# One unread TensorE product behind each unit of a written-out expert layer, in a two-block transformer kernel

## The chip, the cores and the metric

The kernel runs on one core of a Trainium2 chip, as one program launch. The metric is the device time of that launch in microseconds, and what is compared is the median of several runs. TensorE does the matrix products, ScalarE (ACT) and VectorE (DVE) the elementwise work and the reading of PSUM, GpSimd (POOL) one kind of subtraction, and the SyncE queue (SP) issues the loads of weights.

## What is computed

The reference runs two transformer blocks over 256 tokens of width 2048: a first one with matrix LSTM scan, pooling and a gated unit, and a second one with attention, a recurrent branch and a layer of experts. Around the change it is the experts that matter:

```
def peer_ffn(x, w_peer_q, peer_subkeys, peer_u, peer_v):
    ...
    def chunk(args):
        xc, ec, gc = args
        u = peer_u[ec]
        act = jax.nn.gelu(jnp.einsum('tkd,td->tk', u, xc))
        return jnp.einsum('tk,tkd->td', gc * act, peer_v[ec])
```

There are 16384 experts. Each token picks 128 of them (8 heads by 16), and the kernel computes the first expert layer, `gelu(peer_u @ x)`, for all experts and all 256 tokens, then weights the result with a mostly empty table of gates, and multiplies by `peer_v`.

## The kernel before

All weights come through one stream of **units** of 2048 columns by 128 partitions (1 MB). SP loads a unit into one of four `ring` buffers. A unit marked N is split for accuracy: ACT copies each half to `unit_hi` (rounded to the fp32r form that TensorE reads in one pass), POOL subtracts to give `unit_lo`, and TensorE makes three products for each piece of 128 columns: hi by hi, hi weights by lo tokens, lo weights by hi tokens. There are four hi and four lo half-unit buffers, so the split runs up to two units ahead. The semaphores are `hi_done` (ACT to POOL), `lo_done` (POOL to PE), `half_done` (PE to ACT, which also frees the buffers) and `tile_free` (the reader of a PSUM bank to PE).

`STAGES` lists the stages in program order, and `plan()` numbers their units. The experts are handled in two halves, r = 0 and r = 1. Each half has these stages:

- `peer_u{r}`: 64 units. Each unit makes one tile of 128 experts by 256 tokens, with 16 pieces of three products, so 48 products of 256 columns. The tile goes to one of the PSUM banks 0 to 3 in turn. ACT applies the gelu and writes it into `peer_w`.
- for r = 1 only, `pp`: two units, a small projection that VectorE copies out.
- `build`: 32 groups of 16 products of 64 columns in banks 5 and 6 (the gate table, built from `hot` and `hotg`), which VectorE multiplies into `peer_w`.
- `peer_v{r}`: 64 units. Here all 16 pieces of output stay in PSUM over the whole stage, in all eight banks. VectorE then adds banks 0 to 7, one after the other, to `resid`. For r = 0 it raises `acc_used` after bank 3, and again after bank 7.

On TensorE, `run()` calls `iterations()`, which makes a loop (`Fori`) of 15 iterations of four units, and writes out the last four units behind it. Inside a unit, `n_unit()` waits for `lo_done` for each half, waits for `tile_free` before the first product, and raises `half_done` at the last product of each half. Before `peer_u1`, TensorE waits for `acc_used` of 1, since that stage writes banks 0 to 3 alone. It waits for `acc_used` of 2 before the `build` of r = 1. Other stages (`ro`, `wo`, `pq` among them) have patterns of 16 units that are written out, without a loop.

Of the kernel before, what the change touches and what calls it, by code (L numbers as in the profile page):

```python
# [32 lines left out]
P = 128  # L33
T = 256
D = 2048
KC = D // P
# [4 lines left out]
TILES = 4  # L41
# [10 lines left out]
I2 = NKEY // 2  # L52
# [2 lines left out]
NG = KC // GR  # L55
BIG = 3.0e38
GATE_UP = 2.0 ** 15
SCALE = 192.0 ** -0.5


# [100 lines left out]
PLAN, N_UNITS, N_SPLIT = plan()  # L161
# [12 lines left out]
def program(nc, A, out):  # L174
    with ExitStack() as ctx:
# [33 lines left out]
        bank = [ctx.enter_context(nc.psum_tensor(f"bank{i}", [P, 512], F32)) for i in range(8)]  # L209
# [3 lines left out]
        def S(name):  # L213
            if name not in sems:
                sems[name] = ctx.enter_context(nc.semaphore(name))
            return sems[name]
# [4 lines left out]
        tile_free = {"D": S("tile_free_dve"), "A": S("tile_free_act")}  # L221
# [18 lines left out]
        xl = [zone("xl_hi", 0, [P, KC, T], F32R), zone("xl_lo", 16, [P, KC, T], F32R)]  # L240
# [216 lines left out]
        def _(pe):  # L457
# [9 lines left out]
            def n_unit(s, movs, per_tile, it, j):  # L467


                n_tiles = s.tiles // len(movs)  # L470
                n = s.n0 + j + it * s.npi
                for f in range(2):
                    b = (2 * (s.n0 + j) + f) % NBUF
                    pe.wait_ge(lo_done, 2 * n + f + 1)
                    for i in range(8 * f, min(8 * f + 8, n_tiles * per_tile)):
                        t, k = i // per_tile, i % per_tile
                        if s.name == "pg" and j == 0 and k == 3 * GR:
                            ple_sums(0, 3)
                        if s.name in SPLITS and isinstance(it, int) and it == 0 and j == 0 and k % GR == 0:
                            moving_ready(s.name, k // GR)  # L480
                        tile = [(j * n_tiles + t) * len(movs) + m for m in range(len(movs))]
                        if k == 0:

                            pe.wait_ge(tile_free[s.eng], s.base + tile[-1] + 1 + it * (s.npi * s.tiles))
                        for w, x in ((hb, 0), (hb, 1), (lb, 0)):
                            for m, mv in enumerate(movs):
                                mm = pe.matmul(bank[(s.t0 + tile[m]) % TILES][:, 0:T],  # L487
                                               w[b][:, (i % 8) * P:(i % 8 + 1) * P], mv[x][:, k, :],
                                               start=(k == 0 and w is hb and x == 0),
                                               stop=(k == per_tile - 1 and w is lb))  # L490
                    mm.then_inc(half_done, 1)
# [30 lines left out]
            def run(name, movs=None, per_tile=KC, extra=None, mid=None, early=False):  # L522

                s = PLAN[name]

                if s.td:
                    pe.wait_ge(tile_free["D"], TILES + s.td)
                if s.ta and not early:
                    pe.wait_ge(tile_free["A"], TILES + s.ta)

                def body(it, last):
                    j = 0
                    for pos, kind in enumerate(s.pattern):
                        if kind == "P":
                            continue
                        n_unit(s, movs, per_tile, it, j)
                        if extra is not None:
                            extra(it, j)
                        j += 1
                iterations(pe, s, body, mid, 1 if name in SPLITS else 0)  # L540
# [123 lines left out]
            for d in range(2):  # L664
                for t in range(4):
                    mm = pe.matmul(bank[5][:, (d * 4 + t) * 4:(d * 4 + t) * 4 + 4],
                                   gi[:, t * P:(t + 1) * P], ident[0:64, 32 * d:32 * d + 4],
                                   start=True, stop=True, skip_group_check=True)
# [18 lines left out]
            for i in range(2 * NH):  # L687
                pick = ident[0:64, 32 * (i % 2) + i // 2:32 * (i % 2) + i // 2 + 1].to_broadcast([64, P])
                mm = pe.matmul(bank[4 + i // 2][:, (i % 2) * T:(i % 2 + 1) * T], pick, mrow[:], start=True, stop=True,
                               skip_group_check=True)  # L690
# [6 lines left out]
            for g in range(4):  # L697
                for j in range(2):
                    for k in range(2):
# [3 lines left out]
                                       start=(k == 0), stop=(k == 1), skip_group_check=True)  # L703
# [220 lines left out]
            pe.wait_ge(S("pu_ready"), NG)  # L924
            for r in range(2):
                if r == 1:
                    pe.wait_ge(S("acc_used"), 1)
                run(f"peer_u{r}", [xl], mid=(12, gates_tp) if r == 0 else None)
                if r == 1:
                    pe.wait_ge(S("p_ready"), 1)  # L930
                    run("pp", [[pt_r[:, 0, :, :], pt_r[:, 1, :, :]]], per_tile=2)


                def build(it, r=r):
                    for k in range(2):
                        i = r * (T // TG) + k + it * 2
                        pe.wait_ge(S("hot_1"), i + 1)
                        pe.wait_ge(S("hot_g"), i + 1)
                        pe.wait_ge(S("g_used"), i + 1)
                        for t in range(TG):  # L940
                            for x in range(2):
                                mm = pe.matmul(bank[5 + k][:, t * I2:(t + 1) * I2], oa[k][:, :, t], ob[k][:, x, :, t],  # L942
                                               start=(x == 0), stop=(x == 1), skip_group_check=True)
                        mm.then_inc(S("g_done"), 1)
                if r == 1:
                    pe.wait_ge(S("acc_used"), 2)
                with pe.Fori(0, T // TG // 2) as it:
                    build(it)

                s = PLAN[f"peer_v{r}"]  # L950
                pe.wait_ge(tile_free["A"], TILES + s.ta)
                pe.wait_ge(tile_free["D"], TILES + s.td)
                pe.wait_ge(S("g_used"), (r + 1) * (T // TG) + 2)

                def body(it, first, r=r, s=s):
                    for j in range(4):
                        n = s.n0 + j + it * 4
                        pe.wait_ge(S("wr_ready"), r * I2 + j + 1 + it * 4)
                        for f in range(2):
                            b = (2 * (s.n0 + j) + f) % NBUF  # L960
                            pe.wait_ge(lo_done, 2 * n + f + 1)
                            for c in range(8):
                                cc = 8 * f + c
                                o = bank[cc // 2][:, (cc % 2) * T:(cc % 2 + 1) * T]
                                for w_, x in ((hb, 0), (hb, 1), (lb, 0)):
                                    mm = pe.matmul(o, w_[b][:, c * P:(c + 1) * P], wr[j % 2][:, x, :],  # L966
                                                   start=(first and j == 0 and cc % 2 == 0 and w_ is hb and x == 0),
                                                   stop=False, skip_group_check=True)
                            mm.then_inc(half_done, 1)
                body(0, True)  # L970
                with pe.Fori(1, s.iters) as it:
                    body(it, False)
# [1535 lines left out]
```

## Time and profile before

| | |
|---|---|
| time before, median of 3 runs | 4004.07 us |
| lowest and highest of them | 3997.33 and 4007.48 us |
| span of the profiled execution | 3992.3 us |
| instructions in it | 73386 |
| TensorE products, and weight loads | 30508 each |
| PE busy (share of the span) | 3801.4 us (95%) |
| POOL busy | 2894.1 us (72%) |
| DVE busy | 1848.5 us (46%) |
| ACT busy | 1556.9 us (39%) |
| mean granted TensorE clock | 0.967 |

The profile is of one execution, from its first instruction to its last. The run time holds the span and what lies around it, so the table's median is higher than the span. The stage that is changed, `peer_u1`, stands in the span between 3049 and 3413 us.

### The profile page before, as it was taken

The page shows a single profiled execution, that of the slowest core. Times are in us where ns is not written, and L with a number is a line of the kernel's source. Part 1 is how long each engine was busy: PE and PEld are TensorE (multiplying, and loading weights), DVE is VectorE, ACT ScalarE, POOL GpSimd, SP SyncE. Part 2 cuts the span into 40 slices and gives each one's busy share as a digit, 9 for nine tenths or more (in the row PEclk, how much of TensorE's full clock was granted, in tenths as well). Part 3 has the DMA queues.
Part 4 walks back from the last instruction along what each step waited for, and adds up shares of the span by engine and source line. Part 5 has one row for each costly group of instructions (what it writes and reads, how often), then busy time and mean ns, then how long its engine had stood idle before and what let it go on. Part 6 is the DMA issues. An engine that isn't in the chain of part 4 may idle for free.

```text
span 3992.3 us, 73386 instructions
## 1 busy us (share of the span) xinstructions
PE 3801.4 (95%) x30508; PEld 3670.4 (92%) x30508; DVE 1848.5 (46%) x2576; ACT 1556.9 (39%) x1879; POOL 2894.1 (72%) x1146
## 2 busy tenths in 40 slices
PE   6999998899999889999999999999999999999988
PEld 3799998899998879999999999989999999899988
DVE  6685347773425464372025692264442100634445
ACT  5313433333434334454444334414444444144443
POOL 0157965686976738698888798828887888288876
PEclk9999999999999999999999999969999999699999
DMA  8466743463743425345555445515554555145543
GB/s 329 166 264 259 272 183 127 169 231 139 273 169 123 151 83 209 138 169 190 183 188 181 176 179 188 189 53 190 183 184 176 184 189 183 69 169 182 186 148 127
DMA packets 98248, 714.11 MB, mean 179 GB/s; under 512 B 11024, under 2 KB 11152, under 8 KB 12048
## 3 DMA queue, kind: packets, MB, share of 16 engines
q1 hardware_dynamic: 97056, 703.65, 48.2%
q10 hardware_dynamic: 1008, 7.79, 0.5%
q8 instruction: 141, 2.31, 0.2%
q14 instruction: 43, 0.35, 0.0%
HBM read 709.30 MB, written 2.10 MB: 178 GB/s over the span
## 4 chain that ended last, share of the span: by engine, by line
PE 75%; POOL 11%; DVE 8%; issue 3%; ACT 2%; DMA 1%; DVEq 0%; POOLq 0%; SPq 0%; ACTq 0%
PE bank L487 47%; PE bank L966 18%; POOL unit_lo L445 11%; PE bank L942 3%; PE bank L616 1%; DMA ring<-in_w 1%; DVE unit_lo L1582 1%; PE bank L516 1%; PE bank L555 1%; ACT unit_hi L988 1%; PE bank L499 1%; PE bank L725 0%; ACT att_s L1202 0%; PE bank L892 0%; DVE c_raw L1949 0%
## 5 line engine op out<-in xcount | busy, mean ns | idle before, releaser
L445 POOL TENSOR_TENSOR unit_lo<-ring,unit_hi 128x1024 fp32r<-128x1024 f32 x1132 | 2869.2, 2552 | 983.4 <-ACT unit_hi L988 982.0
L988 ACT ACTIVATE unit_hi<-ring 128x1024 fp32r<-128x1024 f32 x1204 | 1239.4, 1055 | 1238.8 <-PE bank L487 543.1
L487 PE MATMUL bank<-xl_hi,unit_hi 128*128 128x256 f32 x4976 | 1405.8, 283 | 50.8 <-POOL unit_lo L445 27.5
L487 PE MATMUL bank<-xl_hi,unit_lo 128*128 128x256 f32 x4976 | 1394.3, 280 | 0.0
L487 PE MATMUL bank<-xl_lo,unit_hi 128*128 128x256 f32 x4976 | 1393.7, 280 | 0.0
L487 PEld LDWEIGHTS bank<-xl_hi,unit_hi 128*128 128x128 f32 x4976 | 940.7, 189 | 62.4 <-issue 26.9
L487 PEld LDWEIGHTS bank<-xl_lo,unit_hi 128*128 128x128 f32 x4976 | 941.3, 189 | 0.5
L487 PEld LDWEIGHTS bank<-xl_hi,unit_lo 128*128 128x128 f32 x4976 | 941.5, 189 | 0.0
L966 PE MATMUL bank<-w_r,unit_hi 128*128 128x256 f32 x4096 | 728.2, 280 | 4.5 <-DVE w_r L2315 4.5
L966 PEld LDWEIGHTS bank<-w_r,unit_hi 128*128 128x128 f32 x4096 | 629.2, 189 | 5.0 <-issue 5.0
L966 PE MATMUL bank<-w_r,unit_lo 128*128 128x256 f32 x2048 | 574.3, 280 | 0.0
L2315 DVE TENSOR_TENSOR w_r<-peer_w,w_r 128x256 fp32r<-128x256 f32 x128 | 290.9, 2273 | 425.9 <-ACT w_r L1329 425.9
L966 PEld LDWEIGHTS bank<-w_r,unit_lo 128*128 128x128 f32 x2048 | 386.9, 189 | 0.0
L1406 DVE SCALAR_TENSOR_TENSOR ada_acc<-ring,cond,ada_acc 128x2048 f32<-128x2048 f32 x64 | 230.7, 3604 | 86.5 <-DMA ring<-in_w 84.9
L1318 ACT ACTIVATE peer_w<-bank 128x256 f32 (+1 forms) x128 | 49.4, 386 | 439.3 <-PE bank L487 439.3
L2296 DVE COPY ple_in<-bank 128x256 f32<-128x256 f32 x16 | 5.7, 418 | 313.2 <-PE bank L487 313.2
L487 PE MATMUL bank<-ry_hi,unit_hi 128*128 128x256 f32 x512 | 142.5, 278 | 2.9 <-DVE h_acc L2166 2.3
L487 PE MATMUL bank<-ry_hi,unit_lo 128*128 128x256 f32 x512 | 142.3, 278 | 0.0
L487 PE MATMUL bank<-ry_lo,unit_hi 128*128 128x256 f32 x512 | 142.1, 278 | 0.0
L487 PE MATMUL bank<-xc_hi,unit_hi 128*128 128x256 f32 x448 | 128.0, 286 | 10.0 <-DVE tick L1534 7.3
L942 PE MATMUL bank<-hotg,hot 128*128 128x64 f16 x1024 | 135.0, 301 | 1.8 <-issue 0.4
L942 PEld LDWEIGHTS bank<-hotg,hot 128*128 128x128 f16 x1024 | 120.2, 147 | 16.1 <-issue 16.1
(415 smaller groups left out, 4979.4 us busy)
## 6 DMA issues: line engine op xcount, KB each, us to landing
ring<-in_w SPq DMA_DIRECT2D x669, 1024.0 KB, 4.8
resid<-in_xT ACTq DMA_DIRECT2D x1, 2048.0 KB, 15.7
tmp_ctx<-in_ctxT ACTq DMA_DIRECT2D x1, 2048.0 KB, 10.6
rnn_gates<-in_rgw ACTq DMA_DIRECT2D x1, 2048.0 KB, 9.1
out<-resid SPq DMA_DIRECT2D x4, 512.0 KB, 2.6
con<-in_con ACTq DMA_DIRECT2D x1, 512.0 KB, 3.2
con<-in_con ACTq DMA_DIRECT2D x1, 448.0 KB, 7.9
p_tmp<-in_pT ACTq DMA_DIRECT2D x1, 256.0 KB, 4.0
```

The costliest lines, as they stand in the source:

```text
L445: pool.tensor_tensor(lb[b][:], ring[slot][:, f * HALF:(f + 1) * HALF], hb[b][:].bitcast(F32), ALU.subtract).then_inc(lo_done, 1)
L487: mm = pe.matmul(bank[(s.t0 + tile[m]) % TILES][:, 0:T], w[b][:, (i % 8) * P:(i % 8 + 1) * P], mv[x][:, k, :], start=(k == 0 and w is hb a ...
L499: mm = pe.matmul(bank[4][:, 64 + b * KC + c:65 + b * KC + c], a[:, c * P:(c + 1) * P], ones[:, 0:1], start=True, stop=True, skip_group_che ...
L516: mm = pe.matmul(bank[(s.t0 + 2 * (j // 4) + t) % TILES][:], xl[x][:, k, t * P:(t + 1) * P], w_[u][:, q * 512:(q + 1) * 512], start=(k == ...
L555: mm = pe.matmul(dst, ones, src[:, k, :], start=(k == 0), stop=(k == n - 1))
L616: mm = pe.matmul(dst[:, m * T:(m + 1) * T], w_[b][:, (i % 8) * P:(i % 8 + 1) * P], mv[x][:, k, :], start=(first and w_ is w[0] and x == 0 ...
L942: mm = pe.matmul(bank[5 + k][:, t * I2:(t + 1) * I2], oa[k][:, :, t], ob[k][:, x, :, t], start=(x == 0), stop=(x == 1), skip_group_check=True)
L966: mm = pe.matmul(o, w_[b][:, c * P:(c + 1) * P], wr[j % 2][:, x, :], start=(first and j == 0 and cc % 2 == 0 and w_ is hb and x == 0), sto ...
L988: act.activation(hb[b][:], ring[slot][:, f * HALF:(f + 1) * HALF], ACT.Copy).then_inc(hi_done, 1)
L1318: act.activation(at_chunk(W, j + it * 4), bank[(s.t0 + j) % TILES][:, 0:T], ACT.Gelu_apprx_tanh).then_inc(tile_free["A"], 1)
L1406: dve.scalar_tensor_tensor(a[:], ring[u % RING][:], col, a[:], ALU.mult, ALU.add).then_inc(plain_done, 1)
L2315: dve.tensor_tensor(wr[j % 2][:, 1, :], at(W, i), wr[j % 2][:, 0, :].bitcast(F32), ALU.subtract).then_inc(S("wr_ready"), 1)
```

## The change

A table `BESIDE` of 64 widths is added: 16 different widths from 8 to 252 columns, each four times, 6752 columns in all. For r = 1 the loop on TensorE is replaced by 64 calls of `n_unit` that are written out. Behind each unit stands one more product. Its weights are a piece of `xl_lo`, its moving operand the first columns of `xl_hi`, as many as the table says, and its result goes to bank 7, where nobody reads it. Since bank 7 is still to be read when `peer_v0` ends, the wait before the stage is now for `acc_used` of 2. No other engine's program is changed.

```
--- before.py
+++ after.py
@@ -55,6 +55,11 @@
+BESIDE = [8, 64, 128, 16, 96, 240, 32, 252, 48, 160, 192, 24, 224, 12, 80, 112,
+          128, 8, 240, 96, 16, 64, 252, 160, 32, 24, 48, 112, 192, 80, 224, 12,
+          96, 16, 8, 252, 128, 32, 64, 48, 240, 112, 24, 80, 160, 12, 192, 224,
+          64, 96, 160, 8, 48, 128, 24, 16, 112, 12, 252, 240, 32, 224, 80, 192]
...
@@ -924,9 +929,17 @@
             pe.wait_ge(S("pu_ready"), NG)
             for r in range(2):
                 if r == 1:
-                    pe.wait_ge(S("acc_used"), 1)
-                run(f"peer_u{r}", [xl], mid=(12, gates_tp) if r == 0 else None)
-                if r == 1:
+                    pe.wait_ge(S("acc_used"), 2)
+                if r == 0:
+                    run("peer_u0", [xl], mid=(12, gates_tp))
+                else:
+                    s = PLAN["peer_u1"]
+                    pe.wait_ge(tile_free["D"], TILES + s.td)
+                    pe.wait_ge(tile_free["A"], TILES + s.ta)
+                    for u in range(I2):
+                        n_unit(s, [xl], KC, u // 4, u % 4)
+                        pe.matmul(bank[7][:, 0:BESIDE[u]], xl[1][:, 0, 0:P], xl[0][:, 0, 0:BESIDE[u]],
+                                  start=True, stop=True, skip_group_check=True)
                     pe.wait_ge(S("p_ready"), 1)
                     run("pp", [[pt_r[:, 0, :, :], pt_r[:, 1, :, :]]], per_tile=2)
```

At the start of the stage, TensorE's program stood like this: the end of `peer_v0` (products from `w_r`), the branch into the loop with its waits, and the first product of the first unit.

```order
15028 L966 MATMUL bank<-w_r_180,unit_lo_60 128x256
15029 L971 REGISTER_ALU
15030 L971 COMPARE_AND_BRANCH
15031 L416 UNCONDITIONAL_BRANCH [waits tile_free_act,tile_free_dve,acc_used]
15032 L416 ISA
15033 L484 REGISTER_ALU [waits lo_done]
15034 L487 MATMUL bank<-xl_hi,unit_hi_53 128x256 [waits tile_free_act]
```

In the changed kernel the same place reads (L492 is the line that was L487, and L979 the one that was L966):

```order
15028 L979 MATMUL bank<-w_r_180,unit_lo_60 128x256
15029 L984 REGISTER_ALU
15030 L984 COMPARE_AND_BRANCH
15031 L492 MATMUL bank<-xl_hi,unit_hi_53 128x256 [waits lo_done,tile_free_act,tile_free_dve,acc_used]
15032 L492 MATMUL bank<-xl_lo,unit_hi_53 128x256
```

The branch and the register work are gone, and the waits stand at the first product. The end of the loop's fourth unit, with the jump back to the first, was this on TensorE:

```order
15233 L487 MATMUL bank<-xl_hi,unit_hi_56 128x256
15234 L487 MATMUL bank<-xl_lo,unit_hi_56 128x256
15235 L487 MATMUL bank<-xl_hi,unit_lo_60 128x256
15236 L416 REGISTER_ALU
15237 L416 COMPARE_AND_BRANCH
15238 L487 MATMUL bank<-xl_hi,unit_hi_53 128x256 [waits tile_free_act,lo_done]
15239 L487 MATMUL bank<-xl_lo,unit_hi_53 128x256
```

In the changed kernel the end of the fourth unit has the added product, 16 columns wide here, between the last product of one unit and the first of the next:

```order
15224 L492 MATMUL bank<-xl_lo,unit_hi_56 128x256
15225 L492 MATMUL bank<-xl_hi,unit_lo_60 128x256
15226 L941 MATMUL bank<-xl_hi,xl_lo 128x16
15227 L492 MATMUL bank<-xl_hi,unit_hi_53 128x256 [waits tile_free_act,lo_done]
15228 L492 MATMUL bank<-xl_lo,unit_hi_53 128x256
```

Nothing else on TensorE moved.

## Rows read from the trace of the kernel before

**Rows 1.** Page, busy time, and shares of the chain that ended last

```profile
PE 3801.4 (95%) x30508; PEld 3670.4 (92%) x30508; DVE 1848.5 (46%) x2576; ACT 1556.9 (39%) x1879; POOL 2894.1 (72%) x1146
...
PE 75%; POOL 11%; DVE 8%; issue 3%; ACT 2%; DMA 1%; DVEq 0%; POOLq 0%; SPq 0%; ACTq 0%
```

**Rows 2.** Busy time in three stretches, with products, clock, DMA; peer_u0's end, peer_u1, ro

```profile
2530.00:2600.00 70.00, 70.00 (x620) 70.00 (x620) 18.36 (x12) 29.86 (x39) 63.28 (x27) 1.00 0.55 195
3100.00:3170.00 70.00, 70.00 (x596) 70.00 (x596) 9.88 (x4) 27.96 (x37) 61.80 (x26) 1.00 0.52 186
1980.00:2050.00 70.00, 70.00 (x620) 70.00 (x619) 13.02 (x30) 29.75 (x30) 63.97 (x27) 1.00 0.55 197
```

**Rows 3.** Who waited for whom in peer_u1, 3052.3 to 3415

```profile
PE bank L487 <- issue: 0.6, 1, 0.6
```

**Rows 4.** VectorE in order of time, 3043 to 3053

```profile
3046.33 2.48 DVE L2321 TENSOR_TENSOR resid<-resid,bank 128x512 f32<-128x512 f32 x4 [7.48 <-PE bank L966]
3048.87 0.06 DVE L1534 MEMSET tick<- 1x1 f32 x1
3048.96 2.48 DVE L2321 TENSOR_TENSOR resid<-resid,bank 128x512 f32<-128x512 f32 x4
3051.50 0.06 DVE L1534 MEMSET tick<- 1x1 f32 x1
```

**Rows 5.** TensorE in order of time, 3045 to 3053

```profile
3049.28 0.58 PE L487 MATMUL bank<-xl_hi,unit_hi 128*128 128x256 f32 x1 [2.99 <-DVE tick L1534]
...
3050.09 0.41 PE L487 MATMUL bank<-xl_hi,unit_hi 128*128 128x256 f32 x1
...
3050.73 0.41 PE L487 MATMUL bank<-xl_hi,unit_hi 128*128 128x256 f32 x1
```

**Rows 6.** The same columns as rows 2, around the stage's start

```profile
3045.42:3048.84 3.42, 0.88 (x8) 1.00 0.75 295
3048.84:3052.25 3.41, 2.97 (x14) 0.50 0.30 77
3052.25:3055.66 3.41, 3.41 (x31) 1.00 0.55 231
```

**Rows 7.** Narrow products in order of time on TensorE

```profile
330.55 3.63 PE L499 MATMUL bank<-con,ada_acc 128*128 128x1 f32 x32
...
2523.60 0.82 PE L922 MATMUL bank<-con,peer_g 128*128 128x128 f32 x6
2524.17 0.36 PE L487 MATMUL bank<-xl_hi,unit_hi 128*128 128x256 f32 x1
2524.37 0.28 PE L487 MATMUL bank<-xl_lo,unit_hi 128*128 128x256 f32 x1
```

**Rows 8.** TensorE in order of time, two restarts behind inserted products

```profile
264.38 0.60 PE L655 MATMUL bank<-con,vstage 128*128 128x128 f32 x4
...
264.94 0.28 PE L487 MATMUL bank<-xc_hi,unit_hi 128*128 128x256 f32 x1
...
265.62 0.28 PE L487 MATMUL bank<-xc_hi,unit_hi 128*128 128x256 f32 x1
...
1602.41 1.02 PE L892 MATMUL bank<-x_conv,rnn_gates 128*128 128x256 f32 x4
...
1603.39 0.28 PE L487 MATMUL bank<-xl_lo,unit_hi 128*128 128x256 f32 x1
```

**Rows 9.** Instruction queue in the written-out stages, 1970 to 2240

```profile
q8 instruction: 18, 0.29, 0.4%
...
ring<-in_w SPq DMA_DIRECT2D x47, 1024.0 KB, 4.8
```

**Rows 10.** End of peer_u1 and start of build, in order of time

```profile
3413.31 0.48 PE L487 MATMUL bank<-p_r,unit_hi 128*128 128x256 f32 x2 [0.63 <-issue]
...
3427.14 3.11 PE L942 MATMUL bank<-hotg,hot 128*128 128x64 f16 x24
```

## The prediction

> **What bounds the kernel now.** I read the busy times and the chain that ended last first: TensorE is busy 95% of the span and carries 75% of the chain [rows 1]. That is a mean over all stages, so next I read the changed stage alone. In `peer_u1` TensorE is busy for 70.00 of 70.00 us, while POOL is busy 61.80 and ACT 27.96 [rows 2]. In the list of waits for the whole stage, TensorE has a single one, 0.6 us at its end [rows 3]. So this stage is bound by TensorE's own stream: what is added to the stream comes out at the end, unless it changes the rate of the rest.
>
> The rate is the second thing to read. The three stretches in [rows 2] are all at the full granted clock, all 70 us long and all without idle time, and yet two of them hold 620 products and `peer_u1` holds 596. Some 2.4 of each count are products in flight at the edges, so the spacing from start to start is 70 / 617.6 = 0.1133 us in the one kind and 70 / 593.6 = 0.1179 us in the other. By the exact starts it is 113.3 and 117.8 ns. The products are the same: 256 columns, fp32r, a new weight load for each. One of the fast stretches is in a loop (`peer_u0`, its last sixteen units), the other in written-out code (`ro`), so it is not the loop that makes the difference. TensorE's stream has **two rates**, and it keeps the one it has until something breaks the series. In the profiled execution the whole of `peer_u1` ran at the slow rate. The difference is 4.44 ns a product, over 64 x 48 = 3072 products 13.65 us. That is more than all that the change adds, and the added products break the series 64 times.
>
> **The change part by part.**
>
> *The 64 added products.* Each brings a weight load of 128 columns and a product of 8 to 252 columns. The trace has no fp32r product as narrow, but it has narrow ones in fp32: 32 products of one column took 3.63 us, of which about 0.26 is the length of the last, and the first two start almost together, so (3.63 - 0.26) / 30 = 112 ns each, and six of 128 columns took 0.82 us [rows 7], (0.82 - 0.27) / 5 = 110 ns each. One column and 128 columns cost the same, so it is the weight load, not the columns, that sets the price. I take 112 ns for each, whatever its width: 64 x 0.112 = 7.2 us. The bounds are 109 ns (the six) and a full place in the slow series with a little for the break, 122 ns: 7.0 to 7.8 us. All of it lies on the path.
>
> The Trainium skill ("TensorE: Matmul & The Clock Gate", the sections on the warm clock's spacing and on LDWEIGHTS) gives a product of N columns N / 2.4 + 2.5 ns, not under about 25 ns, and a weight load its column count / 1.2 ns, which is 107 ns for 128 columns. By the first rule alone the 64 products would cost 6752 / 2.4 + 64 x 2.5 = 2970 ns, 3.0 us. By the second it would be 6.8 us, and the trace's 110 ns side with the second.
>
> *The wait for the second `acc_used`.* TensorE's first product of the stage starts at 3049.28, 2.99 us idle, released by VectorE's event [rows 5]. The event after banks 0 to 3 is at 3048.87, that after banks 4 to 7 at 3051.50 [rows 4]. The new wait is for the later one: 3051.50 - 3048.87 = 2.63 us more idle time. VectorE doesn't depend on TensorE here, so the adds don't move. Queued behind the wait on TensorE is the whole stage, and behind that ACT's gelu, the `half_done` that frees the buffers, and so ACT's and POOL's splits and SP's loads. All of these shift by the same 2.63 us, and nothing catches up, since TensorE has no wait in the stage from which it could be paid. The wait that is saved, before `build`, was long satisfied. Bounds: 2.5 to 2.7 us.
>
> *The clock behind the longer idle time.* At the first products the granted clock is the lower level, 1.2 GHz, for 2.97 us of products, and then it returns to 2.4 GHz [rows 6]. At the low level products are (3050.73 - 3050.09) / 3 = 0.213 us apart [rows 5] instead of 0.118, so a microsecond at the low level costs 0.45 us. With a start at about 3051.9 the next step of the clock, one more stretch like that of [rows 6], would be at 3055.66: 3.75 us at the low level instead of 2.97, which costs 0.35 us more. Bounds: 0, and one further stretch of 3.41 us, 0.35 + 1.5 = 1.9 us. I take 0.35.
>
> *The loop that is written out.* The jump back costs nothing now (no idle time in 330 us of loop, and 70.00 of 70.00 busy in [rows 2]), so nothing is saved. Written-out code must be fetched. In 270 us of written-out stages 18 packets of instructions came for 47 units [rows 9], and a stretch of `ro`, which is among these, is as busy and fast as the fastest loop [rows 2]. I cost it at nothing. The cover is that the fetch runs ahead of TensorE.
>
> *Behind the stage.* `pp` starts after 0.63 us of idle time in which TensorE waited for no other engine, and `build` follows it directly [rows 10]. Neither waits for a thing that now comes earlier, so the shift goes through to the end. POOL's slack (61.80 of 70 us busy, [rows 2]) bears the fast rate as well: at 113.3 ns a unit with its added product takes 5.55 us, and POOL needs 61.80 / 70 x 5.65 = 4.99.
>
> *The rate of the series.* After an inserted product, and after a stall, the series starts anew in one of the two rates. Two cases stand in [rows 8]: behind four products of 128 columns the starts are (265.62 - 264.94) / 6 = 113 ns apart, behind four of 256 columns (1603.86 - 1603.39) / 4 = 118 ns. I followed the starts through the whole trace: of 102 restarts, 15 led into the fast series. Behind stalls and wide insertions the fast one is rare. Behind narrow insertions at the full clock it is four of ten. In the stage there are 64 restarts, four for each width, and the rate may depend on the width or on what the series did before. I take 30% of the units as fast: 0.3 x 13.65 = -4.1 us. The bounds are none (0) and all (-13.65 us).
>
> **The sum.** 7.2 + 2.6 + 0.35 - 4.1 = +6.1 us. The profiled execution's span would go from 3992.3 to 3998.4. What lies around the span (4004.07 - 3992.3 = 11.8 us, against the median of the three runs) stays, so I add the sum to the median: 4010 us, +0.15%.
>
> **The rivals.**
>
> *A: mixed rates,* the forecast, from 10 to 65% of the units fast. The sum goes from 10.15 - 1.4 = +8.8 to 10.15 - 8.9 = +1.3: 4005 to 4013 us. For it: 16 widths will hardly all do the same, and both results are seen behind insertions of the same kind. Chance 0.52.
>
> *B: no unit turns fast.* The added work is paid in full, +10.2 us, 4014 us, and with the upper bounds of the products (7.8) and of the clock (1.9) 7.8 + 2.7 + 1.9 = 12.4, 4016.5. For it: twelve of twelve insertions of the kind at 1602 led back into the slow series. Against it: those are 256 columns wide, wider than any that is added. Chance 0.25.
>
> *C: nearly all units turn fast,* because once in the fast series a narrow insertion keeps it there. 10.15 - 13.65 = -3.5 us, 4000.5 us for all, 4005 at two thirds. For it: the last of the insertions like that at 264 found a fast series and left it fast. Chance 0.15.
>
> *D: faster than before by over 12 us.* `peer_v1`, 3072 products that were slow before too, falls into the fast rate by a draw at its own start, and so do nearly all units of C: another -13.65 us, 3987 us. With A's sum it would be 3996, not enough. Such a draw can hit the kernel before as well, and its run times lie 10 us apart, which it would explain. Chance of both together 0.05.
>
> *E: slower, the written-out stream falls behind.* 64 units need 64 / 47 x 18 = 25 packets of instructions. If each kept TensorE waiting for about a microsecond, that were +25 us on top of B's or A's sum, 4030 us and more. It passes 12 us from about five uncovered packets, with A's sum. Against it: `ro` and its neighbours are written out in just this way and show no such wait. For it: only that the added products and their waits are new to such code. Chance 0.03.
>
> That the change doesn't do what it says is no case of its own: the products stand in TensorE's stream, and nothing removes them.
>
> **How the numbers follow.** About 0.3% (12 us) is what a measurement of this kernel can tell from no change. Slower by over that, above 4016: E whole, and the upper end of B where the clock or the products cost their upper bounds, and a median that is a few microseconds off by the draw of other stages: 0.03 + 0.10 = 0.13. Faster by over that, below 3992: D, 0.05. The rest, 0.82, is within 0.3%. The range takes in A, B's main value and C: 3998 to 4017 us.
>
> **What would show each step.** In the profile after: the first product of the stage starts about 2.6 us after VectorE's first event of the pair, right after the second; the added products take a place of 109 to 122 ns whatever their width, so a unit of 8 columns is no shorter than one of 192; the starts within each unit are 113.3 or 117.8 ns apart, and the share of fast units gives the gain; no wait for instructions lies at the units' borders. It would be wrong if the price of an added product grew with its columns, if a third rate appeared, if products ran slower throughout the stage, or if TensorE began to wait for POOL.

## The result

| | before | changed |
|---|---|---|
| median of the first comparison | 4001.03 us (4 runs) | 4015.26 us (4 runs) |
| ratio, with its 95% interval | | 1.0036 [1.0024, 1.0048] |
| median of a second comparison, five rounds | 4003.97 us (16 runs) | 4015.28 us (11 runs) |
| ratio of the second, with its interval | | 1.0031 [1.0014, 1.0047] |
| span of the profiled execution | 3992.3 us | 4013.1 us |
| last product of `peer_v0` to first of `pp` | 367.29 us | 377.03 us |

The change made the kernel slower by 14.2 us in the first comparison and by 11.3 us in the second, and neither interval holds "no change". The forecast was 4010 us, +0.15%, put down as no change that can be measured. The range of 3998 to 4017 held the time, and what happened is rival B, whose main value was 4014 us.

The changed stage is the last line of the table: +9.74 us. The rest of the 20.8 us between the two spans lies ahead of the stage, in code that did not change. The last product of `peer_v0` starts at 3046.02 us in the profile before and at 3057.00 us in the one after.

The page and the stretches of the changed kernel, with the same columns as [rows 2] (L492 is the line that was L487, L941 the added product; "slow" and "fast" are the two rates of the prediction, 117.8 and 113.3 ns from start to start):

```profile
span 4013.1 us, 73363 instructions
...
PE 3822.4 (95%) x30572; PEld 3691.1 (92%) x30572; DVE 1848.8 (46%) x2576; ACT 1557.0 (39%) x1879; POOL 2893.1 (72%) x1146
```

```profile
3100.00:3170.00 70.00, 70.00 (x597) 70.00 (x596) 12.61 (x7) 28.92 (x39) 59.46 (x25) 1.00 0.50 182
3350.00:3420.00 70.00, 70.00 (x597) 70.00 (x597) 0.00 (x0) 27.58 (x36) 58.12 (x26) 1.00 0.52 188
```

TensorE is still busy without a break in `peer_u1`, and POOL now has 58 to 59 us of work in 70 where [rows 2] has 61.8. A unit now takes 2% longer, and the rest of the difference is what falls into 70 us at the edges (25 or 26 subtractions of about 2.4 us). The count of products, 597, is again that of the slow series, not the 620 of the fast one. The list of waits of the stage, 3064 to 3436, still has nothing for TensorE but the half microsecond at its end, as [rows 3] had:

```profile
PE bank L492 <- issue: 0.5, 1, 0.5
```

The stage's start in order of time, first VectorE (as [rows 4]), then TensorE (as [rows 5]):

```profile
3059.85 0.06 DVE L1547 MEMSET tick<- 1x1 f32 x1
3059.95 2.48 DVE L2334 TENSOR_TENSOR resid<-resid,bank 128x512 f32<-128x512 f32 x4
3062.48 0.06 DVE L1547 MEMSET tick<- 1x1 f32 x1
```

```profile
3057.00 0.28 PE L979 MATMUL bank<-w_r,unit_lo 128*128 128x256 f32 x1
3062.59 0.58 PE L492 MATMUL bank<-xl_hi,unit_hi 128*128 128x256 f32 x1 [5.31 <-DVE tick L1547]
3062.97 0.41 PE L492 MATMUL bank<-xl_lo,unit_hi 128*128 128x256 f32 x1
```

The first product now follows the second event instead of the first. The idle time is 5.31 us instead of 2.99. That is 2.32 us more, where the sum had 2.63: the product now starts 0.05 us after the event has ended, and in the kernel before it started 0.35 us after it, with the branch into the loop in between. The clock is at its lower level from then until 3066.34, 3.75 us, as the sum had it (columns as in [rows 6]):

```profile
3062.59:3066.34 3.75, 3.75 (x17) 0.50 0.60 251
```

Two of the added products, one of 8 columns and one of 252, in the same columns:

```profile
3069.91 0.28 PE L492 MATMUL bank<-xl_hi,unit_lo 128*128 128x256 f32 x1
3070.03 0.17 PE L941 MATMUL bank<-xl_hi,xl_lo 128*128 128x8 f32 x1
3070.05 0.37 PE L492 MATMUL bank<-xl_hi,unit_hi 128*128 128x256 f32 x1
3070.26 0.28 PE L492 MATMUL bank<-xl_lo,unit_hi 128*128 128x256 f32 x1
```

```profile
3110.27 0.28 PE L492 MATMUL bank<-xl_hi,unit_lo 128*128 128x256 f32 x1
3110.39 0.28 PE L941 MATMUL bank<-xl_hi,xl_lo 128*128 128x252 f32 x1
3110.51 0.28 PE L492 MATMUL bank<-xl_hi,unit_hi 128*128 128x256 f32 x1
3110.62 0.28 PE L492 MATMUL bank<-xl_lo,unit_hi 128*128 128x256 f32 x1
```

Count from the last product ahead to the `xl_lo` product behind. It takes 0.35 us in both, where two products of the series take 0.236. The narrow product lets the next one start 0.02 us later, but that one then has 0.37 us in its record and its own follower waits. The weight loads (PEld) around the narrow product show the order: its own load starts with the product ahead of it, at 3069.91, and the load of the next unit's first product starts with the narrow product itself, at 3070.03.

```profile
3069.91 0.19 PEld L941 LDWEIGHTS bank<-xl_hi,xl_lo 128*128 128x128 f32 x1
3070.03 0.19 PEld L492 LDWEIGHTS bank<-xl_hi,unit_hi 128*128 128x128 f32 x1
3070.14 0.19 PEld L492 LDWEIGHTS bank<-xl_lo,unit_hi 128*128 128x128 f32 x1
```

Measured by exact starts, an added product between two units costs 111.9 ns in the mean: 109 to 114 for widths up to 224, 116 to 120 for 240 and 252. The last one costs nothing: the first product of `pp` starts 0.91 us after the unit's last product, with an added product between them as without. The second profile of the changed kernel gives the same figures for each width within a nanosecond, and the same stage within 0.2 us, 377.21 us.

### The profile page after: what moved, and what is told of

It reads as the page before. It is cut to its first block, busy times and chain, and to the rows that moved or that the text cites. A ratio compares the mean times of both kernels' runs of the same rounds, so it can differ in the third digit from the quotient of the medians.

```text
span 4013.1 us, 73363 instructions
## 1 busy us (share of the span) xinstructions
PE 3822.4 (95%) x30572; PEld 3691.1 (92%) x30572; DVE 1848.8 (46%) x2576; ACT 1557.0 (39%) x1879; POOL 2893.1 (72%) x1146
## 4 chain that ended last, share of the span: by engine, by line
PE 75%; POOL 12%; DVE 7%; issue 3%; ACT 2%; DMA 1%; DVEq 0%; POOLq 0%; SPq 0%; ACTq 0%
PE bank L492 46%; PE bank L979 18%; POOL unit_lo L450 12%; PE bank L955 3%; PE bank L621 1%; DVE unit_lo L1595 1%; PE bank L521 1%; PE bank L560 1%; DMA ring<-in_w 1%; ACT unit_hi L1001 1%; PE bank L504 0%; PE bank L730 0%; ACT att_s L1215 0%; PE bank L897 0%; PE bank L598 0%
## 5 line engine op out<-in xcount | busy, mean ns | idle before, releaser
L492 PE MATMUL bank<-xl_hi,unit_hi 128*128 128x256 f32 x4976 | 1412.0, 284 | 52.6 <-POOL unit_lo L450 28.3
L492 PE MATMUL bank<-xl_lo,unit_hi 128*128 128x256 f32 x4976 | 1396.7, 281 | 0.0
L492 PE MATMUL bank<-xl_hi,unit_lo 128*128 128x256 f32 x4976 | 1396.1, 281 | 0.0
L492 PEld LDWEIGHTS bank<-xl_hi,unit_hi 128*128 128x128 f32 x4976 | 943.2, 190 | 64.3 <-POOL unit_lo L450 25.7
L492 PEld LDWEIGHTS bank<-xl_lo,unit_hi 128*128 128x128 f32 x4976 | 942.7, 189 | 0.5
L492 PEld LDWEIGHTS bank<-xl_hi,unit_lo 128*128 128x128 f32 x4976 | 942.6, 189 | 0.0
L979 PE MATMUL bank<-w_r,unit_hi 128*128 128x256 f32 x4096 | 728.1, 281 | 4.5 <-DVE w_r L2328 4.5
L979 PEld LDWEIGHTS bank<-w_r,unit_hi 128*128 128x128 f32 x4096 | 628.8, 189 | 5.0 <-issue 5.0
L979 PE MATMUL bank<-w_r,unit_lo 128*128 128x256 f32 x2048 | 573.3, 280 | 0.0
L979 PEld LDWEIGHTS bank<-w_r,unit_lo 128*128 128x128 f32 x2048 | 386.1, 189 | 0.0
L492 PE MATMUL bank<-ry_hi,unit_hi 128*128 128x256 f32 x512 | 143.5, 280 | 2.9 <-DVE h_acc L2179 2.3
L492 PE MATMUL bank<-ry_hi,unit_lo 128*128 128x256 f32 x512 | 143.1, 279 | 0.0
L492 PE MATMUL bank<-ry_lo,unit_hi 128*128 128x256 f32 x512 | 142.9, 279 | 0.0
L492 PE MATMUL bank<-xc_hi,unit_hi 128*128 128x256 f32 x448 | 128.5, 287 | 10.0 <-DVE tick L1547 7.3
```

What stands on the lines that cost most here:

```text
L492: mm = pe.matmul(bank[(s.t0 + tile[m]) % TILES][:, 0:T], w[b][:, (i % 8) * P:(i % 8 + 1) * P], mv[x][:, k, :], start=(k == 0 and w is hb a ...
```

## The experiments

What each tests is read in the profile as the time from the last product of `peer_v0` to the first of `pp` ("the stage"), and as the period of a unit. Both are free of what happens elsewhere. The bare unit in the slow series has 48 x 117.8 = 5.653 us.

**Repeat of the changed kernel.** No edit.

> The changed kernel itself once more, in five rounds beside the kernel before. My theory (the change's own cost is 9.9 us, products 7.2, wait 2.6 and a little, and the rest of the 14.2 us between the first medians was the draws of other stages): +9 to +12 us, a ratio of 1.0023 to 1.0030. Rival (the change costs more outside its stage): +14 us or more, 1.0035 and up.

Measured: 4015.28 us against 4003.97, +11.3 us, ratio 1.0031 [1.0014, 1.0047]; the stage 377.21 us. That fits the change's own cost, and doesn't exclude 14 us.

**The wait alone.**

```
                 if r == 1:
-                    pe.wait_ge(S("acc_used"), 1)
+                    pe.wait_ge(S("acc_used"), 2)
```

> The kernel before with one edit: the wait ahead of peer_u1 is for the second acc_used, the loop stays, no product is added. My theory (each part of the change costs what it shows in the trace): the first product of the stage starts 2.3 to 2.7 us later behind the last of peer_v0 (5.6 us from start to start instead of 3.26), the low clock takes up to 0.4 us more or less, and the stage from peer_v0's last product to pp's first is 369 to 371 us instead of 367.3. Rival (the later start costs more than its own length, by the clock): 371 to 373 us. The whole time: +2.5 us, which the draws of the other stages (some 4 us either way) will blur.

```profile
3060.84 0.57 PE L487 MATMUL bank<-xl_hi,unit_hi 128*128 128x256 f32 x1 [5.61 <-DVE tick L1534]
```

Measured: the stage 369.91 us, +2.62 over the kernel before, where the events lie 2.63 us apart [rows 4]. The clock came back 2.93 us after the first product, no later than in [rows 6], so here the longer idle time cost its own length and nothing more. In the eight other profiles with the late wait it came back 3.15 to 4.24 us after it. The whole time was 4011.21 us against 4004.07, ratio 1.0015 [0.9998, 1.0033]: too blurred to tell +2.6 us from nothing or from twice as much.

**Written out alone.** The early wait, no products:

```
                     for u in range(I2):
                         n_unit(s, [xl], KC, u // 4, u % 4)
-                        pe.matmul(bank[7][:, 0:BESIDE[u]], xl[1][:, 0, 0:P], xl[0][:, 0, 0:BESIDE[u]],
-                                  start=True, stop=True, skip_group_check=True)
```

> The changed kernel without the 64 products and with the early wait: the stage is written out and nothing else. My theory: no cost, the stage is 367 to 368 us in the slow series, or 353 to 354 if it falls into the fast one by its draw. Rival (the written-out stream costs by fetches or by the waits at its products): more than 369 us, up to the 10 us that the changed kernel's stage is longer than before.

Measured: the stage 363.68 us, 3.6 us less than before, total 4005.91 against 4004.07, ratio 1.0005 [0.9992, 1.0017]. Writing out costs nothing; 22 packets of instructions came in 330 us of the changed kernel's stage and none held TensorE up. The gain of 3.6 us has three parts. The stage began in the fast series and left it in its tenth unit, after 456 products: 456 x 4.44 ns = 2.0 us. The granted clock stayed at its upper level over the stage's start, behind 2.69 us of idle time, where [rows 6] has 2.97 us at the lower one. At the 0.45 us that a microsecond there costs by the starts in [rows 5], that is 1.3 us. And without the branch into the loop the first product starts 0.3 us earlier. The start of the stage, in the columns of [rows 6]:

```profile
3055.03:3058.44 3.41, 3.41 (x30) 1.00 0.33 84
```

The rows around the place where the fast series ends, in order of time:

```profile
3106.59 0.28 PE L492 MATMUL bank<-xl_lo,unit_hi 128*128 128x256 f32 x1
3106.70 0.28 PE L492 MATMUL bank<-xl_hi,unit_lo 128*128 128x256 f32 x1
3106.82 0.30 PE L492 MATMUL bank<-xl_hi,unit_hi 128*128 128x256 f32 x1
3106.96 0.28 PE L492 MATMUL bank<-xl_lo,unit_hi 128*128 128x256 f32 x1
3107.08 0.28 PE L492 MATMUL bank<-xl_hi,unit_lo 128*128 128x256 f32 x1
```

Starts 0.11 us apart, one of 0.14, and from then on 0.12. The weight load that belongs to the product at 3106.82 begins some 37 ns late. It is the first of a half unit, the one that waits for POOL, and VectorE was building its tables at the same time: the four subtractions of POOL from 3100.89 took 11.16 us, 2.79 each instead of the 2.42 of the stage's mean. The second of them ended at 3106.69. Counted by half units from the program's end, it is the one that this product needs, and its weight load was due at 3106.70. That a wait of a few hundredths of a microsecond for POOL ended the fast series is inferred from this; no record names it.

**Two products for each one.**

> The changed kernel with two unread products of the same width behind each unit. My theory (an added product is a weight load of 112 ns whatever its width): a unit's period goes from 5.765 to 5.877 us, the stage from 377 to 384 us. Rival (the price is the break of the series, paid once a unit): the period stays near 5.77 us. Rival (a second narrow product falls on another phase): some units in the fast series, periods of 5.67 us.

Measured: the stage 384.00 us, +6.97 over the changed kernel. The mean period went from 5.765 to 5.878 us, 112 ns for each further product, with single periods of 5.79 to 5.98 us and every unit at 117.8 ns. Total 4021.51 us, ratio 1.0035 [1.0014, 1.0056]. The price is paid for each product, not once for each break.

**Fewer weight columns.**

```
-                        pe.matmul(bank[7][:, 0:BESIDE[u]], xl[1][:, 0, 0:P], xl[0][:, 0, 0:BESIDE[u]],
+                        m = 8 * (u // 4) + 8
+                        pe.matmul(bank[7][0:m, 0:16], xl[1][:, 0, 0:m], xl[0][:, 0, 0:16],
```

> The changed kernel with an added product of 16 columns whose weights have 8 columns behind units 1 to 4, 16 behind units 5 to 8, and so on to 128: the weight load is shortened, not the product. My theory: the price is that of the weight load, so a unit's period grows with the weight columns from about 5.68 us (a floor of some 25 to 30 ns) to 5.765 at 128, and since the place in time at which the series goes on differs, some units turn to 113.3 ns. Rival (the price is fixed for each product): 5.765 us for all, and all units at 117.8 ns. Rival (a shorter load delays the next one): periods above 5.765.

Measured: 5.760 us a unit with 8 weight columns, 5.766 with 128. So the product costs 107 to 113 ns even where its own weight load is a sixteenth. My expectation failed, and the rival of a fixed price stood.

**Four products, half of the units with short weight loads.** The rival left two readings: each product has a fixed price, or the price is that of the *next* unit's weight load. In the rows above, that load starts only with the narrow product, and a narrow product is too short to cover it. The second reading is called theory L.

```
+                        m = 8 if u < 32 else P
+                        for _ in range(4):
+                            pe.matmul(bank[7][0:m, 0:16], xl[1][:, 0, 0:m], xl[0][:, 0, 0:16],
```

> The changed kernel with four unread products of 16 columns behind each unit; for units 1 to 32 their weights have 8 columns, for units 33 to 64 128. Theory L (the price is the weight load that follows a narrow product and is not covered by it): in the first half the first three are followed by a load of 8 columns, cheap (25 to 50 ns each), and only the last by one of 128, so a period of 5.84 to 5.91 us; in the second half 4 x 0.109 more than the bare 5.653, 6.09 us. Rival (each product has a fixed price of some 107 ns, whatever it loads): 6.08 us in both halves.

```profile
3091.56 0.28 PE L492 MATMUL bank<-xl_hi,unit_lo 128*128 128x256 f32 x1
3091.68 0.25 PE L943 MATMUL bank<-xl_hi,xl_lo 128*8 128x16 f32 x4
3091.78 0.36 PE L492 MATMUL bank<-xl_hi,unit_hi 128*128 128x256 f32 x1
3091.99 0.28 PE L492 MATMUL bank<-xl_lo,unit_hi 128*128 128x256 f32 x1
```

```profile
3401.32 0.28 PE L492 MATMUL bank<-xl_hi,unit_lo 128*128 128x256 f32 x1
3401.43 0.51 PE L943 MATMUL bank<-xl_hi,xl_lo 128*128 128x16 f32 x4
3401.80 0.36 PE L492 MATMUL bank<-xl_hi,unit_hi 128*128 128x256 f32 x1
3402.00 0.28 PE L492 MATMUL bank<-xl_lo,unit_hi 128*128 128x256 f32 x1
```

With 8 weight columns four products take 0.25 us and the period is 5.843 us, 0.190 over the bare unit. With 128 they take 0.51 us and the period is 6.100, 0.447 over it. The last of the four is followed by a load of 128 columns in both halves (107 ns, from the run before), so the other three cost (190 - 107) / 3 = 28 ns each where a load of 8 columns follows, and about 112 where one of 128 does. Theory L holds: the price of a narrow product is the weight load behind it. Two widths of that load were tried, 8 and 128 columns, and none between. The Trainium skill ("TensorE: Matmul & The Clock Gate", the sections "Back-to-back issue gap" and "LDWEIGHTS (loading the stationary operand)") has both numbers, an issue floor of about 25 ns and, as weight columns over 1.2, 107 ns for 128 of them. The rows are near both, 28 and 107 to 112. Which of them rules is decided by the weight load that follows.

**Other kinds of insertion,** eight units each.

> The changed kernel with other kinds of insertion, eight units each: one, two and four fp32 transposes of 128 columns, one fp32 product of 128 columns, one of 1 column, one fp16 product of 64 columns, one fp32r product of 384 columns, one of 512. My theory (fp32r insertions bring the series back to where it was, fp32 ones of 128 columns shift it): some of the units 1 to 32 run at 113.3 ns from product to product, none of the units 49 to 64. Rival (the rate behind an insertion is chance): fast units in all groups alike. Rival (no insertion changes it in this stage): all 64 at 117.8 ns. Price of the wide ones: 160 ns for 384 columns and 215 for 512, since the product itself is then the longer part.

| insertion | period of a unit, us | over 5.653, ns | fast units |
|---|---|---|---|
| one fp32 transpose of 128 | 5.767 | 114 | 0 |
| two | 5.873 | 220 | 0 |
| four | 6.093 | 440 | 0 |
| one fp32 product of 128 columns | 5.880 | 227 | 0 |
| one of 1 column | 5.880 | 227 | 0 |
| fp16, 64 columns | 5.827 | 174 | 2 of 8 |
| fp32r, 384 columns | 5.827 | 174 | 0 |
| fp32r, 512 columns | 5.890 | 237 | 0 |

The fp32 ones didn't shift the series, against my expectation; the fp16 one did twice. A fast unit was followed by a slow one each time, behind the next insertion. An fp32 product shows two records, each at the price of a weight load, whether it has 1 column or 128.

**fp16 insertions of other widths,** eight units each.

> The changed kernel with fp16 insertions (weights from the fp16 table of places) of 8, 16, 32, 96, 128, 160, 192 and 256 columns, eight units each, since the fp16 one of 64 columns was the only kind behind which a unit ran in the fast series (two of eight). Theory (an fp16 weight load is shorter, so the next load starts at another point of time, which is what decides the series): fast units behind several of the widths below about 128, in a fixed pattern of 8, and none behind those of 160 and more, where the product covers the load. Rival (chance at two in eight): fast units in all groups. Rival (64 columns is special): none.

Measured: three fast units in all, one behind an insertion of 96 columns, one behind 128, one behind 192, each of them followed by a slow unit. Neither theory of a pattern holds. Three of 64 is what a draw gives.

**Does a narrow insertion end a fast series?** The first try had fp16 products to make the series fast and narrow fp32r ones behind.

> Behind units 1, 5, 9 and so on the fp16 product of 64 columns, behind units 3, 7, 11 and so on the fp32r one of 64 columns as in the changed kernel, behind the others nothing. It asks what a narrow fp32r insertion does to a series that is fast. My theory (it restarts the series slow, whatever it was): some three to five of the 16 pairs behind the fp16 product run at 113.3 ns, both units of the pair alike, and every pair behind the fp32r product at 117.8. Rival (the fp32r one keeps the series as it is): pairs behind it are fast where the pair ahead was.

No unit of the 64 was fast, so it said nothing. The second try went to stages where the series is fast now and then, and left `peer_u1` alone:

```
+            def beside(mv):
+                def extra(it, j):
+                    if j % 4 == 3:
+                        pe.matmul(bank[7][:, 0:64], mv[1][:, 0, 0:P], mv[0][:, 0, 0:64], start=True, stop=True,
+                                  skip_group_check=True)
+                return extra
-            run("ro", [ry])
+            run("ro", [ry], extra=beside(ry))
```

and the same for `ga`, `yr`, `gr`, `wo` and `peer_u0`.

> The kernel before (peer_u1 as it was) with one fp32r product of 64 columns behind every fourth unit of other stages: ga, yr, gr, ro, wo and peer_u0, 36 in all. There the series is fast now and then by its own draw, so this shows what a narrow fp32r insertion does to a fast series. My theory (it restarts the series at the slow rate): each such insertion that meets a fast series is followed by 117.8 ns. Rival (it keeps the rate that it meets): 113.3 ns ahead and behind. Price where the series is slow on both sides and TensorE doesn't wait: 0.112 us each.

> The same kernel as e9_elsewhere once more, since it is a matter of chance in which stages the series is fast. The same two expectations: behind an insertion that meets 113.3 ns, 117.8 by my theory, 113.3 by the rival. If neither run has a fast series that meets an insertion, the question stays open.

There are 36 insertions in each run. Three met a fast series, two in the first run and one in the second, and behind all three it was slow. One of them, in order of time:

```profile
2421.86 0.28 PE L487 MATMUL bank<-xl_hi,unit_lo 128*128 128x256 f32 x1
2421.97 0.28 PE L487 MATMUL bank<-xl_hi,unit_hi 128*128 128x256 f32 x1
2422.09 0.28 PE L487 MATMUL bank<-xl_lo,unit_hi 128*128 128x256 f32 x1
2422.20 0.28 PE L487 MATMUL bank<-xl_hi,unit_lo 128*128 128x256 f32 x1
2422.32 0.19 PE L903 MATMUL bank<-xl_hi,xl_lo 128*128 128x64 f32 x1
2422.34 0.37 PE L487 MATMUL bank<-xl_hi,unit_hi 128*128 128x256 f32 x1
2422.55 0.28 PE L487 MATMUL bank<-xl_lo,unit_hi 128*128 128x256 f32 x1
2422.67 0.28 PE L487 MATMUL bank<-xl_hi,unit_lo 128*128 128x256 f32 x1
```

Ahead of it (2422.20 - 2421.86) / 3 = 0.113 us, behind it 117.8 ns over the next 37 products by exact starts. In the first of the three the stage `ro` was fast for four units, until its first insertion; in [rows 2] the same stage stayed fast throughout. My theory holds on three cases, but only where the stream runs on. Behind three other insertions the series was fast, and each time TensorE had to wait between the insertion and the next unit: twice 0.21 us for POOL, and once 0.58 us at the start of `ro`:

```profile
1976.33 0.19 PE L903 MATMUL bank<-xl_hi,xl_lo 128*128 128x64 f32 x1
1977.10 0.36 PE L487 MATMUL bank<-ry_hi,unit_hi 128*128 128x256 f32 x1 [0.58 <-issue]
1977.30 0.28 PE L487 MATMUL bank<-ry_lo,unit_hi 128*128 128x256 f32 x1
1977.41 0.28 PE L487 MATMUL bank<-ry_hi,unit_lo 128*128 128x256 f32 x1
1977.52 0.28 PE L487 MATMUL bank<-ry_hi,unit_hi 128*128 128x256 f32 x1
1977.64 0.28 PE L487 MATMUL bank<-ry_lo,unit_hi 128*128 128x256 f32 x1
```

## Why the prediction was right or wrong

**What bounds the stage** was right: TensorE stayed busy all the time, and what was added came out at the end.

**The 64 products** were sized right, at 112 ns against 111.9 measured, though 63 are paid and not 64, since the last one lies in the time that `pp` waits anyway. The reason given was half right. "The weight load, not the columns" is true, but it is not the product's own load, which is hidden under the product ahead. It is the load that follows. The two can't be told apart in rows where all loads have 128 columns, as those of [rows 7] do, and the run with shorter weights refuted the one reading. One row was also misread. Line 499 makes one product for each of 16 pieces, so the 32 records of one column in [rows 7] are 16 fp32 products of two records each, as the fp32 products of the table above have. Such a product costs 224 ns, and 112 ns is the price of one record, that is of one weight load. The figure fits an fp32r product because that has one load; the six transposes, with one record each, bear it out at 110 ns.

**The wait** was right: 2.63 us by the two events, 2.62 measured alone. **The clock** was right in this profile (3.75 us at the lower level) and near it in the other one of the changed kernel (4.1 us, from 3062.57 to 3066.71), and it costs nothing in the run with the wait alone. But the 2.97 us of the kernel before, from which the term is counted, are themselves a draw. With the early wait, behind 2.69 to 3.02 us of idle time, the clock was at the lower level at the stage's start in two of four profiles, for 2.97 and 3.41 us, and in the two others not at all. With the late wait, behind 5.31 to 5.61 us, it was there in all nine, for 2.93 to 4.24 us. The means are 1.6 and 3.6 us, so an estimate of what the late wait costs by the clock is 2.0 x 0.45 = 0.9 us, not 0.35.

**The written-out loop** cost nothing inside the stage, as assumed, and rival E didn't come. At its entry it saved 0.3 us, which the prediction left out: from the last product of `peer_v0` to the first of the stage it is 3.26 us in the kernel before and 2.97 us in the run written out alone, and 5.89 against 5.59 us with the late wait.

**The rate of the series** is the step that failed. It was sized at 30% of the units, -4.1 us. It was 0 of 64 units in both profiles of the changed kernel, and 0 in the runs with two and with four products, so the term is nothing. The choice leaned on four of ten restarts behind narrow insertions in one profile. But these were fp32 insertions, of other shapes, and one place counted among them shows how little it says. The sixteen units of `peer_u0` behind the six transposes [rows 7] are fast in the profile before and in the changed kernel's first one. In the nine other profiles of kernels with the same code there, the repeat of the changed kernel among them, they are slow. Without this term the sum is 7.2 + 2.6 + 0.35 = +10.2 us. The stage measured +9.74, and the difference is the 0.3 us at the loop's entry and the 0.1 us of the last product.

**From 9.74 to 11.3 and 14.2 us.** The 1.5 us between the stage and the second, larger comparison are well within its interval. A part is likely real, since the profile before doesn't show what its kernel does in the mean. The clock, by the estimate above, adds 0.9 - 0.35 = 0.55 us. The other part is the chance of a fast series, which the change takes away. Of five profiles whose stage has no added products (before, the wait alone, written out alone, and the two with insertions elsewhere) one had it, for 2.0 us, which is 0.4 us in the mean. With both the estimate is 9.74 + 0.55 + 0.4 = +10.7 us. It rests on draws in four to nine profiles, so it is argued, not shown. The five stages are 367.3 (before), 367.3 (the wait alone, less its 2.6), 363.7 (written out alone), 367.5 and 366.0 us (insertions elsewhere). That of 366.0 us is slow throughout, and is shorter because the clock stayed at its upper level:

```profile
3074.38:3077.80 3.42, 3.41 (x29) 1.00 0.40 125
```

The further 3 us of the first comparison are best taken as draws ahead of the stage. Over eleven profiles the last product of `peer_v0` starts anywhere from 3046.0 to 3061.3 us, in kernels whose code up to there is the same, while all that comes behind the stage takes 578.2 to 579.6 us. The profile before, on which the prediction rests, had the earliest start of all.

That the time fell into the range is in part luck. The forecast was 4.1 us too low by the rate, and 5 us below the measured median. The range held it because it took in B's main value, and because it was counted from a median of 4004.07 us, while the kernel before had 4001.03 us in the comparison. Against that median the change cost 14.2 us, more than the 12 us that the prediction called measurable.

The line between "no change" and "slower" at 0.3% lay at 4013 to 4016 us, and the change's own cost plus these draws sits close to it. The first comparison lies beyond the line of 12 us and the second just within. The chance of 0.13 for slower was too small for that reason: it came from B's extremes, where B's main value was already near the line.

## What to carry to other kernels

An fp32r product that is too narrow to cover the weight load behind it costs that load, whatever its own width and its own weights: between products with 128 weight columns it is about 112 ns, and its own columns add nothing up to 224. That is shown for following loads of 8 and 128 columns. A trace can show a rate that an unchanged kernel takes only by chance. Before such a rate, or a lower clock behind a short idle time, goes into a forecast, compare the same place in several profiles, not several places in one. And an early wait on the first half of a buffer's readers can be worth microseconds, here 2.6, that a later wait on all of them gives away in silence.

## What the runs showed of the hardware that was not expected

- The same written-out or looped series of fp32r products of 256 columns has two rates, 113.3 and 117.8 ns from start to start, at the same granted clock of 1.00. It stays at one over hundreds of products and changes mostly at breaks, by what looks like chance: the place behind the six transposes was fast in 2 of 11 profiles. Why there are two is open. Where the stream ran on behind a narrow fp32r product, the slow one followed (63 of 63 units in each of the two profiles of the changed kernel, and three of three that met a fast series). With a wait of 0.21 to 0.58 us behind it, it was fast three times. A half unit that seems to have come late ended a fast series once.
- Narrow products with 8 weight columns follow each other at 28 ns, and with 128 at 112.
- Idle times of 2.69 and 3.02 us ahead of the stage left the granted clock at 1.00, and two of 2.99 us were followed by 2.97 and 3.41 us at 0.50. Behind 5.31 to 5.61 us it was 0.50 in nine of nine profiles.
- An fp16 product of 64 columns between fp32r ones costs 174 ns, more than an fp32r product of 252 (120 ns), and its columns don't change that from 8 to 256. What it waits for is open.
- No version was found that beats the kernel before. The fast series would be worth up to 13.65 us in this stage, but nothing that was tried leads into it or holds it reliably.
